# Keys and values of tiles 0 and 1 loaded and projected ahead of the queries, and groups of transposes and scores placed together

## What is computed

```python
h = rms_norm(x, norm1_g)
[u | q | k | v] = h @ w_in        # 512 | 512 | 128 | 128 columns
a = pool_mixer(u)                 # trailing means over 2, 4, 8, 16 frames, minus u, mapped and scaled
b = swa_sink_attention(q, k, v)   # 8 query heads, 2 key/value heads, chunks of 64, window 128,
                                  # QK norm, ALiBi, one sink per head
x = x + concat(a, b) @ w_out
x = x + square(relu(rms_norm(x, norm2_g) @ w_up)) @ w_down
```

## Time and profile before

| what | us |
|---|---|
| median of 3 runs | 864.29 (864.01 to 866.1) |
| profiled execution, its own time | 863.61 |
| its span, first to last instruction | 861.80 |
| PE busy | 856.5 (99% of the span) |
| DVE busy | 539.3 (63%) |
| ACT busy | 416.4 (48%) |
| POOL busy | 233.8 (27%) |
| granted TensorE clock, mean | 1.00 of full speed |

### The profile page before, as it was taken

The page is one execution under the profiler, slowest core; times in us unless marked ns, Lnnn a source line. Parts: engine busy times, 40 slices in busy tenths (PEclk is TensorE's granted clock), DMA queues, the critical chain, the costliest instruction groups (busy, mean ns, idle before and its releaser), DMA issues.

```text
span 861.8 us, 10784 instructions
## 1 busy us (share of the span) xinstructions
PE 856.5 (99%) x4062; PEld 709.0 (82%) x4062; DVE 539.3 (63%) x741; ACT 416.4 (48%) x728; POOL 233.8 (27%) x195
## 2 busy tenths in 40 slices
PE   8999999999999999999999999999999999999998
PEld 7888888888888888888888888888888888888887
DVE  7788588844477765666566566458745464646462
ACT  8865446632157555555555555534333333333330
POOL 2421201010141222234322223004543004444440
PEclk9999999999999999999999999999999999999999
DMA  9531002651011654445554442899742453242422
GB/s 349 177 124 48 26 25 74 212 204 48 26 49 50 229 174 134 135 169 178 156 170 135 135 135 94 309 373 359 264 173 94 167 190 121 98 141 96 146 99 72
DMA packets 67598, 128.37 MB, mean 149 GB/s; under 512 B 3529, under 2 KB 20187, under 8 KB 67547
## 3 DMA queue, kind: packets, MB, share of 16 engines
q1 hardware_dynamic: 67376, 127.55, 43.3%
q10 hardware_dynamic: 171, 0.14, 0.0%
HBM read 89.92 MB, written 37.75 MB: 148 GB/s over the span
## 4 chain that ended last, share of the span: by engine, by line
PE 99%; DMA 1%; DVE 0%; ACT 0%; SPq 0%; issue 0%
PE bank L1503 31%; PE bank L1505 31%; PE bank L1504 31%; PE bank L1666 1%; PE bank L1682 1%; PE bank L1516 1%; PE bank L1635 1%; DMA mem<-in_w_in 1%; PE bank L1615 0%; PE bank L1538 0%; PE bank L1529 0%; PE bank L1534 0%; DVE wgt L1075 0%; ACT wgt L680 0%; PE bank L1619 0%; PE bank L1628 0%
## 5 line engine op out<-in xcount | busy, mean ns | idle before, releaser
L1503 PE MATMUL bank<-b_op,s_op 128*128 128x512 f32 (+1 forms) x450 | 174.7, 388 | 0.0
L1504 PE MATMUL bank<-b_op,s_op 128*128 128x512 f32 (+1 forms) x450 | 174.6, 388 | 0.0
L1505 PE MATMUL bank<-b_op,s_op 128*128 128x512 f32 (+1 forms) x450 | 174.6, 388 | 0.0
L1259 DVE TENSOR_TENSOR s_op<-s_in,s_op 128x1024 fp32r<-128x1024 f32 x56 | 75.9, 1356 | 125.6 <-ACT s_op L850 125.5
L625 POOL TENSOR_TENSOR b_sum<-d_raw,d_raw 128x1024 f32<-128x1024 f32 x40 | 96.9, 2422 | 201.2 <-DVE b_op L1263 201.2
L850 ACT ACTIVATE s_op<-s_in 128x1024 fp32r<-128x1024 f32 x56 | 59.4, 1060 | 177.4 <-PE bank L1505 151.2
L1220 DVE TENSOR_TENSOR ring<-raw,ring 128x512 fp32r<-128x512 f32 x96 | 87.4, 924 | 34.0 <-ACT ring L798 32.7
L1503 PE MATMUL bank<-xs,ring 128*128 128x512 f32 x256 | 99.7, 389 | 0.0
L1505 PE MATMUL bank<-xs,ring 128*128 128x512 f32 x256 | 99.6, 389 | 0.0
L1504 PE MATMUL bank<-xs,ring 128*128 128x512 f32 x256 | 99.6, 389 | 0.0
L1503 PEld LDWEIGHTS bank<-b_op,s_op 128*128 128x128 f32 x450 | 84.5, 188 | 17.8 <-DVE b_op L1263 0.4
(11 more groups left out here) (166 smaller groups left out, 1419.5 us busy)
## 6 DMA issues: line engine op xcount, KB each, us to landing
s_in<-h_keep SPq DMA_DIRECT2D x56, 512.0 KB, 4.0
h_keep<-h_set SPq DMA_DIRECT2D x16, 1280.0 KB, 5.1
raw<-in_w_up SPq DMA_DIRECT2D x16, 1024.0 KB, 6.4
d_raw<-in_w_down SPq DMA_DIRECT2D x32, 512.0 KB, 7.7
mem<-in_x SPq DMA_DIRECT2D x16, 512.0 KB, 5.1
h_keep<-h_set SPq DMA_DIRECT2D x16, 512.0 KB, 4.6
x_keep<-mem SPq DMA_DIRECT2D x8, 512.0 KB, 3.5
mem<-x_keep SPq DMA_DIRECT2D x8, 512.0 KB, 7.1
```

What stands on the lines that cost most here:

```text
L1259: nc.vector.tensor_tensor(out=s_op[G % 3][:, LO], in0=s_in[G % 3], in1=s_op[G % 3][:, HI].bitcast(F32), op=ALU.subtract).then_inc(op_lo, 1)
L1503: nc.tensor.matmul(out_ap, lhs[HI], rhs[HI], start=first, stop=False, skip_group_check=chained)
L1504: nc.tensor.matmul(out_ap, lhs[HI], rhs[LO], start=False, stop=False, skip_group_check=chained)
L1505: return nc.tensor.matmul(out_ap, lhs[LO], rhs[HI], start=False, stop=last, skip_group_check=chained)
```

## The change

- Loads: x_T of tiles 0 and 1 come in halves; keys' and values' columns come first, in five transfers (k 0, k 1, then pairs, `KV_LOADS`), the queries' columns after them, in eight. The order is x_T(0) first half, kv 0, kv 1, x_T(1) first half, kv 2 and 3, both second halves, kv 4 and 5, kv 6 and 7, q 0 to 7, x(0).
- Splits on ACT and DVE in the same order. ACT's last two `slope_rows` move behind them. `copy_kv(0)` waits for all low parts.
- PE: `project_first_kv` projects keys and values of tiles 0 and 1, `project_first_q` queries of tile 0, then `project_q(1)`. `spin(6)` becomes `spin(4)`.
- PE's order later: `transpose_in(0)`, `score(0)`, `transpose_in(1)`, `turn_rinv(0)`, `transpose_probs(0)` come after one to three more blocks k; `score(2)` moves behind `project_kv(4, range(6))`, next to `attend(1)`; `transpose_in(5)` and `transpose_in(7)` move next to a `transpose_probs`.
- ACT: `take_rinv(0)` ahead of both groups of `exponentials(0)`. DVE: `attention_low(0)` two steps earlier; in `pooled` one semaphore in place of two.
- `down(0, 0)`: the HI x HI and LO x HI passes of the first four tiles run before the wait for `b_op`'s low part, the four HI x LO passes after it.

```diff
@@ -192,11 +195,12 @@
+KV_LOADS = (range(0, 1), range(1, 2), range(2, 4), range(4, 6), range(6, 8))
 cols_in, constants_in, x_tok_in = sem("cols_in"), sem("constants_in"), sem("x_tok_in")
 xT_in = [sem(f"xT_in{i}") for i in range(2)]
-xT_first_in = sem("xT_first_in")
+xT_first_in = [sem(f"xT_first_in{i}") for i in range(2)]
 resid_in = [sem(f"resid_in{i}") for i in range(NT)]
-w_qkv_in = [sem(f"w_qkv_in{k}") for k in range(KT)]
+w_kv_in = [sem(f"w_kv_in{i}") for i in range(len(KV_LOADS))]
 w_u_in = [sem(f"w_u_in{j}") for j in range(KT // 2)]
@@ -204,9 +208,11 @@
 h_first_kept, h_rest_kept = ([sem(f"{n}{i}") for i in range(2)] for n in ("h_first_kept", "h_rest_kept"))
-d_in = {q: [sem(f"d_in_{q}_{i}") for i in range(8)] for q in ("B11", "B12", "B22")}
+w_q_and_B22_in = [sem(f"w_q_and_B22_in{i}") for i in range(KT)]
+d_in = {q: [sem(f"d_in_{q}_{i}") for i in range(8)] for q in ("B11", "B12")}
+d_in["B22"] = w_q_and_B22_in
 d_in["B21"] = d_in["B12"]
-D_LANDED = {"B11": 16, "B12": 16, "B22": 16, "B21": 32}
+D_LANDED = {"B11": 16, "B12": 16, "B22": 32, "B21": 32}
 s_in_landed = [sem(f"s_in_landed{i}") for i in range(3)]
@@ -250,14 +256,11 @@
-KV_COLS, Q_COLS, QKV_COLS = slice(Q_W, QKV_W), slice(0, Q_W), slice(0, QKV_W)
-
-def qkv_pieces(k):
-    return (KV_COLS, Q_COLS) if k == 0 else (QKV_COLS,)
+KV_COLS, Q_COLS = slice(Q_W, QKV_W), slice(0, Q_W)
 def qkv_count(k, cols):
-    return 1 + k + (1 if k or cols == Q_COLS else 0)
+    return 1 + k + (KT if cols == Q_COLS else 0)
@@ -273,7 +276,7 @@
-FIRST_XT = [(0, 0), (0, 1), (1, 0), (1, 1)]
+FIRST_XT = [(0, 0), (1, 0), (0, 1), (1, 1)]
@@ -344,8 +346,14 @@
-    def load_w_qkv(k):
-        sp.dma_start(w_qkv_stage[k], w_in_k[k][:, POOL_W:IN_W]).then_inc(w_qkv_in[k], 16)
+    def load_w_kv(i):
+        ks = KV_LOADS[i]
+        dst = w_qkv_stage[ks[0]] if len(ks) == 1 else w_kv_pair[ks[0]]
+        src = w_in_k[ks[0]] if len(ks) == 1 else w_in_pair[ks[0] // 2]
+        sp.dma_start(dst[..., KV_COLS], src[..., POOL_W + Q_W:IN_W]).then_inc(w_kv_in[i], 16)
+    def load_w_q(k):
+        sp.dma_start(w_qkv_stage[k][:, Q_COLS], w_in_k[k][:, POOL_W:POOL_W + Q_W]).then_inc(w_q_and_B22_in[k], 16)
@@ -405,13 +413,17 @@
-    load_xT_half(0)
-    for k in range(KH):
-        load_w_qkv(k)
-    load_xT_half(1)
-    for k in range(KH, KT):
-        load_w_qkv(k)
-    load_xT(1)
+    load_xT_half(0, 0)
+    load_w_kv(0)
+    load_w_kv(1)
+    load_xT_half(1, 0)
+    load_w_kv(2)
+    for t in range(2):
+        load_xT_half(t, 1)
+    load_w_kv(3)
+    load_w_kv(4)
+    for k in range(KT):
+        load_w_q(k)
     load_x(0)
@@ -674,11 +686,15 @@
-    def split_w_qkv(k):
-        sc.wait_ge(w_qkv_in[k], 16)
-        for cols in qkv_pieces(k):
-            nc.scalar.activation(w_qkv_s[:, k, HI, cols], w_qkv_stage[k][:, cols], ACT.Copy,
-                                 scale=g1[:, k:k + 1]).then_inc(w_qkv_hi, 1)
+    def split_w_kv(k):
+        sc.wait_ge(w_kv_in[next(i for i, ks in enumerate(KV_LOADS) if k in ks)], 16)
+        nc.scalar.activation(w_qkv_s[:, k, HI, KV_COLS], w_qkv_stage[k][:, KV_COLS], ACT.Copy,
+                             scale=g1[:, k:k + 1]).then_inc(w_qkv_hi, 1)
+    def split_w_q(k):
+        sc.wait_ge(w_q_and_B22_in[k], 16)
+        nc.scalar.activation(w_qkv_s[:, k, HI, Q_COLS], w_qkv_stage[k][:, Q_COLS], ACT.Copy,
+                             scale=g1[:, k:k + 1]).then_inc(w_qkv_hi, 1)
@@ -706,6 +722,8 @@
             sc.wait_ge(kT_done, t)
+        else:
+            sc.wait_ge(w_qkv_lo, 2 * KT)
         sc.wait_ge(kv_done, t + 1)
@@ -866,15 +884,20 @@
     x_high(0, (0,))
+    sc.wait_ge(setup_dve, COLS_READY)
+    for k in range(2):
+        split_w_kv(k)
+    x_high(1, (0,))
+    for k in range(2, KH):
+        split_w_kv(k)
+    for t in range(2):
+        x_high(t, (1,))
+    for k in range(KH, KT):
+        split_w_kv(k)
+    for k in range(KT):
+        split_w_q(k)
     slope_rows(2)
     slope_rows(3)
-    sc.wait_ge(setup_dve, COLS_READY)
-    for k in range(KH):
-        split_w_qkv(k)
-    x_high(0, (1,))
-    for k in range(KH, KT):
-        split_w_qkv(k)
-    x_high(1)
     sum_squares_x(0)
@@ -896,9 +919,8 @@
     head_squares(2)
-    exponentials(0, (0,))
     take_rinv(0)
-    exponentials(0, (1,))
+    exponentials(0)
     x_high(4)
@@ -1293,14 +1313,19 @@
     x_low(0, (0,))
-    for k in range(KH):
-        split_w_qkv(k)
-    x_low(0, (1,))
+    for k in range(2):
+        split_w_qkv(k, KV_COLS)
+    x_low(1, (0,))
+    for k in range(2, KH):
+        split_w_qkv(k, KV_COLS)
+    for t in range(2):
+        x_low(t, (1,))
     for k in range(KH, KT):
-        split_w_qkv(k)
-    x_low(1)
-
-    dve.wait_ge(w_qkv_lo, KT + 1)
+        split_w_qkv(k, KV_COLS)
+    for k in range(KT):
+        split_w_qkv(k, Q_COLS)
+    dve.wait_ge(w_qkv_lo, 2 * KT)
     nc.vector.memset(keys_T[:, 0:CHUNK], 0.0).then_inc(zeroed, 1)
@@ -1354,9 +1379,9 @@
     pooled(0, 2)
+    attention_low(0)
     pooled_low(0, 1)
     scale_u(0, 3)
-    attention_low(0)
     softmax_head(2)
@@ -1517,28 +1542,53 @@
+    def first_kv(t, k, x_part, w_part):
+        if (x_part, w_part) == (HI, HI):
+            pe.wait_ge(xT_hi, xT_count(t, k // KH))
+            pe.wait_ge(w_qkv_hi, qkv_count(k, KV_COLS))
+        elif x_part == LO:
+            pe.wait_ge(xT_lo, xT_count(t, k // KH))
+        else:
+            pe.wait_ge(w_qkv_lo, qkv_count(k, KV_COLS))
+        stop = k == KT - 1 and w_part == LO
+        last = nc.tensor.matmul(bank[KV_B[t]][:, 0:KV_W], act(x_part, k // KH, t)[:, k % KH, :],
+                                w_qkv_s[:, k, w_part, KV_COLS], start=k == 0 and (x_part, w_part) == (HI, HI),
+                                stop=stop)
+        if stop:
+            last.then_inc(kv_done, 1)
+    def project_first_kv():
+        for ks in (range(2), range(2, KH), range(KH, KT)):
+            for k in ks:
+                first_kv(0, k, HI, HI)
+                first_kv(0, k, LO, HI)
+                if k >= 2:
+                    first_kv(1, k, HI, HI)
+                    first_kv(1, k, LO, HI)
+                    first_kv(0, k, HI, LO)
+                    first_kv(1, k, HI, LO)
+            if ks == range(2):
+                for k in ks:
+                    first_kv(0, k, HI, LO)
+                for k in ks:
+                    first_kv(1, k, HI, HI)
+                for k in ks:
+                    first_kv(1, k, HI, LO)
+                for k in ks:
+                    first_kv(1, k, LO, HI)
+    def project_first_q():
         for k in range(KT):
             first, stop = k == 0, k == KT - 1
+            pe.wait_ge(w_qkv_hi, qkv_count(k, Q_COLS))
+            for part in (HI, LO):
+                nc.tensor.matmul(bank[Q_B[0]][:, :], act(part, k // KH, 0)[:, k % KH, :],
+                                 w_qkv_s[:, k, HI, Q_COLS], start=first and part == HI, stop=False)
+            pe.wait_ge(w_qkv_lo, qkv_count(k, Q_COLS))
+            last = nc.tensor.matmul(bank[Q_B[0]][:, :], act(HI, k // KH, 0)[:, k % KH, :],
+                                    w_qkv_s[:, k, LO, Q_COLS], start=False, stop=stop)
+        last.then_inc(q_done, 1)
@@ -1692,23 +1742,24 @@
     nc.tensor.transpose(bank[QT_B][:, 0:P], cols_rows, ident).then_inc(cols_turned, 1)
-    spin(6)
-    project_first()
-    project_kv(1, range(KT))
+    spin(4)
+    project_first_kv()
+    project_first_q()
     project_q(1, range(KT))
-    project_kv(2, range(3))
+    project_kv(2, range(4))
     transpose_in(0)
-    project_kv(2, range(3, KT))
-    project_q(2, range(4))
+    project_kv(2, range(4, KT))
+    project_q(2, range(5))
     score(0)
-    project_q(2, range(4, KT))
+    project_q(2, range(5, KT))
+    project_u(0, 0, range(2))
     transpose_in(1)
-    project_u(0, 0, range(5))
+    project_u(0, 0, range(2, 6))
     turn_rinv(0)
-    project_u(0, 0, range(5, KT))
-    project_u(0, 1, range(5))
+    project_u(0, 0, range(6, KT))
+    project_u(0, 1, range(6))
     transpose_probs(0)
-    project_u(0, 1, range(5, KT))
+    project_u(0, 1, range(6, KT))
     score(1)
@@ -1717,8 +1768,8 @@
     project_u(0, 3, range(KT))
+    project_kv(4, range(6))
     score(2)
-    project_kv(4, range(6))
     attend(1)
@@ -1746,8 +1797,8 @@
     project_kv(6, range(KT))
+    project_q(6, range(3))
     transpose_in(5)
-    project_q(6, range(3))
     transpose_probs(4)
@@ -1765,8 +1816,8 @@
     project_out(0, range(2, 5))
+    project_out(1, range(4))
     transpose_in(7)
-    project_out(1, range(4))
     transpose_probs(6)
@@ -1822,16 +1873,31 @@
         G = p * NG + g
+        tiles = [(j, st) for j in range(2) for st in range(4)]
+        if G == 0:
+            pe.wait_ge(dve_read, 3 * (NCK - 1))
+            pe.wait_ge(act_read, 4 * (NCK - 1))
+            pe.wait_ge(op_hi, 2)
+            pe.wait_ge(op_lo, 1)
+            for st in range(4):
+                for part in (HI, LO):
+                    nc.tensor.matmul(bank[DOWN_BANK[0][st]][:, :], s_op[0][:, part, 0, st * P:(st + 1) * P],
```

(13 more changed lines are left out.)

## The result

| | before | after |
|---|---|---|
| median, us | 864.10 (863.39 to 866.10, 20 runs) | 865.49 (864.06 to 867.15, 20 runs) |
| ratio after / before | | 1.0015, interval 1.0009 to 1.0021 |
| profiled execution, us | 863.61 | 867.15, and in a second profile 866.11 |
| its span, us | 861.8 | 865.3, and 864.3 |

That is inside the 0.3% that I called "the same", but it lies on the other side of my 863.7, at the upper end of the range. The changed kernel's runs also scatter more, and the profiled execution was the longest of its 20.

What follows compares the result with a forecast made beforehand. PE, busy 99% of the span, was taken as the bound. Gains of 0.1 (opening), 0.2 (`score(2)`) and 0.3 us (`down(0)`) sum to 0.6, against the median 864.29: 863.7 us, range 861.9 to 865.6.

Steps and rivals of the forecast that it cites:

- the same: Whole kernel: a time between 861.7 and 866.9 us, within 0.3% (2.6 us) and not told from no change; chance 0.91.
- The step that failed: Opening on PE: up to 2.1 us gained, tile 1 ended near 22.0 us, then a wait for `x_low(2)`.
- the idle stretch ahead of tile 2: PE before tile 2's first matmul: 1.5 to 2 us idle, released by DVE's `x_low`.
- The bound and the anchor: Opening: ACT's chain from the squares, started by x(0)'s landing, sets tile 2; at most 0.8 of 2.1 us survives.
- the cover: Ahead of tile 2: `x_low(2)`'s first half is done 0.85 us before PE needs it at 24.09 us.
- The loads: Opening DMA: smaller weight pieces land x(0) 0.8 us later, 0.5 to 2.9 at the bounds.
- my 350: Opening DMA: rate in GB/s taken for the 1 KB key and value pieces, costing 0.5 us.
- Added waits: `copy_kv(0)` on ACT also waits for the last DVE split, about 16.5 against 17.71 us: cover 1 us.
- `score(2)`: PE, `score(2)` placed next to `attend(1)`: one block entry and one exit less, 0.2 us gained.
- `down(0)`: PE's seam at `down(0)`: eight matmuls hide the wait for `b_op`'s low half, 0.3 us gained.
- Transposes, `take_rinv`, `pooled`: Later transposes on PE, `take_rinv(0)` ahead of the exponentials on ACT, merged semaphore in `pooled`: 0 us each.
- Slower: small pieces: Rival, opening DMA: 1 KB pieces run at 205 GB/s, x(0) lands up to 2.9 us late, 865.1 us; chance 0.20.

Runs made afterwards that it cites:

- e5: Changed kernel with 16 idle matmuls between tile 0's and tile 1's first keys and values on PE; 865.46 us, ratio 1.0017 to the kernel before.
- e9: Changed kernel with the same 16 idle matmuls and two of ACT's slope rows moved ahead of x_T(1)'s first split; 865.11 us, ratio 1.0010 to the kernel before.
- e6: Kernel before with 512 KB of unused loads put between x_T(1) and x(0) in the queue; 864.74 us, ratio 1.0005.
- e2: Kernel before with each 384 KB weight load issued as its 1 KB and 2 KB pieces, splits and PE's order untouched; 865.31 us, ratio 1.0015.
- e8: Changed kernel unaltered, timed and profiled a second time; 865.18 us, ratio 1.0009 to the kernel before.
- e7: Changed kernel with PE's opening order alone undone: tile 0's queries ahead of tile 1's keys and values; 867.63 us, ratio 1.0034 to the kernel before.
- e12: Opening of the kernel before with all the rest of the change, run a second time; 864.01 us, ratio 0.9996 to the kernel before.
- e1: Opening of the kernel before (loads, splits, first projections, spins) with all the rest of the change; 863.87 us, ratio 0.9995 to the kernel before.
- e10: Kernel before with each 384 KB weight load issued as two loads of 64 partitions, pieces still 3 KB; 868.32 us, ratio 1.0051.
- e11: Kernel before with an unused load of 512 bytes issued behind each 384 KB weight load; 864.01 us, ratio 0.9995.

## Why the prediction was wrong, point by point

- **The step that failed: PE ready for tile 2 at 22.0 us, waiting there for `x_low(2)`.** I gave the new opening up to 2.1 us on PE, because keys and values of two tiles need only 1 MB of weights. They also need 1 MB of x_T, half of it of tile 1, which PE had needed only at 15.7 us before and now needs at 6.3. It came at 8.4 and 7.3. PE stood still for 2.3 and 1.3 us, ran some 26 and 24 matmuls at the lower clock behind that, and was at tile 2 at 27.76 and 26.45, without a wait: 3.7 and 2.4 us later than before in place of 2.1 earlier. Even with the clock held it was ready at 25.2 and 24.7 (e5, e9). I had named a clock below 1.00 only behind the idle stretch ahead of tile 2, and that stretch never came.
- **The bound and the anchor: right.** Tile 2's start carries the opening, the squares start as x(0) lands (e6, e9, and both profiles of the changed kernel), and the cover is 0.79 us for 0.85 (e5 and e9).
- **The loads: mis-sized, by their start.** I put x(0) 0.8 us late; it was 3.0 and 1.9 us late, and 1.1 to 1.6 in e2, where the loads alone are cut. I had set the 205 GB/s of `raw(0)` aside because that load starts from an idle queue and ours lie in the middle of a full one. The first of ours don't: they are the first transfers of the kernel, and 2.6 and 1.5 us were lost by the time that 1.05 MB had landed. The window estimates above say the same, some 180 GB/s for the 1 KB pieces up to 8 us and some 370 from there on; my 350 held only for the full queue. 290 GB/s, the point where the change loses, was worked out rightly from a single rate, and a single rate is what the loads did not have. The Trainium skill ("DMA: Bandwidth & Descriptors", Bandwidth) says to batch transfers to 1 MiB or more, and so spoke against cutting these. The cut of e2 did cost 1.0 us, as its direction says; whether by the size of the loads or by the length of their pieces no run here shows, and in the full queue the 256 KB loads of the changed kernel reached 385 GB/s.
- **Added waits.** The last DVE split ended at 17.7 us in e8 (10.63 + 7.09), not 16.5, against `copy_kv(0)` at 19.65: cover enough, no cost. What I had not seen is `copy_q(0)` behind PE (1.1 and 1.3 us); e7 shows that it followed from the rest.
- **`score(2)`: right** in place and size (0.18 for 0.2). **`down(0)`: right** (0.32 for 0.3), but 0.15 is given back at the next group, for which I had no term. **Transposes, `take_rinv`, `pooled`: right**, 0: between 80 and 550 us e12 keeps its distance to the kernel before.
- **The rivals.** "Slower: small pieces" (865.1, chance 0.20) has the time, and its sign came true (234 to 238 GB/s in 4 to 7 us, tile 2 behind 25 us). Its mechanism is half of what happened: x(0) was late by 1.9 to 3.0 us, as it says, but not at one rate of 205 GB/s, and PE was later still, so that the chain behind x(0) did not set tile 2. That the time fits is in part luck. Sum by the runs: the medians give +1.0 for the cut loads (e2) and -0.4 for the rest (e1), 0.6; measured 1.4, and 0.8 in e8's group. The rest of 0.2 to 0.8 us is left to the new order in the opening (standstill, clock, splits at the end), and the smaller of these is not clear of noise; I can't part it further, since the two profiled executions lie at 867.15 and 866.11, above the median.

What stays open: some executions of the changed kernel take 864.1 us and others 866.2, and none of the short ones was profiled. In its two profiles there is also a stall of 0.2 to 0.4 us in the up products near 290 us, not in e12; and one of the 16 transfer engines ended its share of an opening load 1.1 us behind the others in the first profile and in e9. Why the transfer engines are unused in part at 4 to 5 us (share 0.66 with 134 GB/s in the row above), and why the first loads suffer more than the later ones, isn't shown either.

The best version is the rest of the change with the opening as it was (e1, e12): 0.35 us less by the traces, too little for the medians to prove.

## What to carry over

A rate read where the queue is full doesn't price the first loads of a kernel: loads cut to bring the wanted columns first can make everything behind them late, those columns included. Count all that the new order needs early, the activations too, not only the weights. When one load gets later, follow every consumer in the new order of work, not only the one that set the end before; and when a gap in PE is closed by reordering, ask what PE's clock does if a gap opens elsewhere. A gain at one seam has to be checked against the next seam: what follows may have had just as little cover.

## What was unexpected of the hardware

- 3 KB pieces to 64 partitions moved 275 GB/s with the transfer engines full, to 128 partitions 417 (e10 and the kernel before, 8 to 12 us).
- The column of the granted clock can read 1.00 while matmuls start 0.21 us apart in place of 0.12, the distance of 1.2 GHz (e8, 9 to 13.5 us). e12 reads 1.00 with pairs 0.64 apart in place of 0.35 (6 to 9 us). The distance between starts is the surer reading.
- A low half of `b_op` that ended 0.05 us before PE's matmul started still went with 0.11 us lost: that matmul shows 0.50 us for 0.39 (559.54 in e12), as in the earlier trace rows.
- Eight more loads of 512 bytes, issued between those of 384 KB, had no effect on the landings (e11).
